# Rotation of the rotary vectors moved from TensorE to VectorE in blocks of 32 rows, and latent attention taken by pairs of heads

## The reference

```python
# differential attention, layer 1 of the first block: q and k have 8 heads x 2 maps x 64 values
q_l = apply_rope(rms_norm(q...), cos, sin); k_l = apply_rope(rms_norm(k...), cos, sin)
# latent attention (_mla), 8 heads, 16 meta tokens + 256 tokens = 272 positions
q = (_rmsnorm(q_lat, q_lat_w) @ w_uq).reshape(B, L, 8, 128 + 64)      # per head: 128 "nope", 64 rotary
kv = (_rmsnorm(kv_lat, kv_lat_w) @ w_ukv).reshape(B, L, 8, 128 + 128)
q_pe = _rope(_rmsnorm(q_pe, qpe_w), cos, sin)
k_pe = _rope(_rmsnorm(k_pe, kpe_w), cos, sin)                          # one rotary key for all heads
s = einsum(q_nope, k_nope) + einsum(q_pe, k_pe)
p = softmax(s * (128 + 64) ** -0.5); o = p @ v                         # then times silu(gate), out projection
# _rope / apply_rope on the halves x1, x2 (32 values each) of a 64-vector:
out = concatenate([x1 * cos - x2 * sin, x2 * cos + x1 * sin])
```

## Time and profile before

| | |
|---|---|
| median of 3 runs | 1290.42 us (1289.99 to 1291.06) |
| the profiled execution's own time | 1291.02 us |
| its span in the trace | 1289.3 us |
| mean granted TensorE clock | 0.984 of full speed |
| PE busy | 1225.1 us, 95% |
| DVE busy | 679.0 us, 53% |
| ACT busy | 549.8 us, 43% |

### The profile page before, as it was taken

One profiled execution on the slowest core, in us unless ns is written; L12 is line 12 of the kernel. 1 busy time (PEld: TensorE's weight loads), 2 busy tenths in 40 slices (PEclk: granted clock), 3 DMA queues, 4 the chain that ended last, 5 costly groups with the idle time before them and its releaser, 6 DMA issues.

```text
span 1289.3 us, 18951 instructions
## 1 busy us (share of the span) xinstructions
PE 1225.1 (95%) x7202; PEld 1002.7 (78%) x7202; DVE 679.0 (53%) x1141; ACT 549.8 (43%) x1026; POOL 87.2 (7%) x124
## 2 busy tenths in 40 slices
PE   7999999999999997999988899999899989999998
PEld 5765787787788885789946899999797675798467
DVE  3444477676433336555196754455664434355743
ACT  3234322222132224544366644444565554466742
POOL 0012011122000001000000200000100000020500
PEclk9999999999999998999989999999999999899899
DMA  9889265678422221323310465554353321363011
GB/s 326 307 309 325 87 196 184 198 263 277 155 98 98 92 87 50 98 77 121 99 34 1 131 196 191 174 184 152 123 179 100 96 89 45 75 201 142 33 43 56
DMA packets 121367, 183.40 MB, mean 142 GB/s; under 512 B 4305, under 2 KB 92672, under 8 KB 121296
## 3 DMA queue, kind: packets, MB, share of 16 engines
q1 hardware_dynamic: 113744, 154.64, 36.2%
q0 software_dynamic: 7552, 27.80, 6.8%
HBM read 181.37 MB, written 1.05 MB: 141 GB/s over the span
## 4 chain that ended last, share of the span: by engine, by line
PE 84%; DVE 7%; ACT 4%; issue 3%; POOL 1%; DMA 0%; DVEq 0%; SPq 0%; ACTq 0%; POOLq 0%
PE ps L440 20%; PE ps L442 20%; PE ps L441 20%; PE ps L751 2%; PE ps L791 2%; PE ps L752 2%; PE ps L753 2%; PE ps L920 2%; PE ps L933 2%; PE ps L1910 1%; PE ps L1954 1%; DVE wl L425 1%; PE ps L2242 1%; PE ps L2244 1%; PE ps L2243 1%
## 5 line engine op out<-in xcount | busy, mean ns | idle before, releaser
L425 DVE TENSOR_TENSOR wl<-raw,wh 128x1024 fp32r<-128x1024 f32 (+2 forms) x242 | 294.8, 1220 | 271.6 <-ACT wh L420 269.1
L440 PE MATMUL ps<-hh,wh 128*128 128x256 f32 (+3 forms) x1256 | 420.8, 335 | 17.1 <-DVE hl L570 11.4
L441 PE MATMUL ps<-hl,wh 128*128 128x256 f32 (+3 forms) x1256 | 412.1, 328 | 0.0
L442 PE MATMUL ps<-hh,wl 128*128 128x256 f32 (+3 forms) x1256 | 411.1, 327 | 0.0
L420 ACT ACTIVATE wh<-raw 128x1024 fp32r<-128x1024 f32 (+2 forms) x242 | 251.9, 1043 | 278.3 <-PE ps L442 256.5
L440 PEld LDWEIGHTS ps<-hh,wh 128*128 128x128 f32 (+1 forms) x1256 | 239.6, 191 | 57.3 <-issue 27.7
L442 PEld LDWEIGHTS ps<-hh,wl 128*128 128x128 f32 (+1 forms) x1256 | 239.7, 191 | 20.8
L441 PEld LDWEIGHTS ps<-hl,wh 128*128 128x128 f32 (+1 forms) x1256 | 238.9, 190 | 21.0 <-issue 0.2
L440 PE MATMUL ps<-ah,wh 128*128 128x256 f32 (+3 forms) x400 | 134.0, 335 | 5.5 <-DVE al L1751 3.0
L441 PE MATMUL ps<-al,wh 128*128 128x256 f32 (+3 forms) x400 | 131.9, 330 | 0.0
L442 PE MATMUL ps<-ah,wl 128*128 128x256 f32 (+3 forms) x400 | 131.7, 329 | 0.0
(11 more groups left out here) (209 smaller groups left out, 1474.8 us busy)
## 6 DMA issues: line engine op xcount, KB each, us to landing
raw<-in_ffn_w_in SPq DMA_DIRECT2D x44, 1024.0 KB, 5.1
raw<-in_ffn_w_out SPq DMA_DIRECT2D x22, 1024.0 KB, 4.9
raw<-in_w_in SPq DMA_DIRECT2D x22, 1024.0 KB, 5.4
big<-in_w_ada SPq DMA_DIRECT2D x16, 1024.0 KB, 9.7
big<-in_w_ada POOLq DMA_DIRECT2D x24, 512.0 KB, 4.4
ex<-in_w_ada POOLq DMA_DIRECT2D x24, 512.0 KB, 5.0
raw<-in_diff_w_in SPq DMA_DIRECT2D x12, 1024.0 KB, 5.1
raw<-in_w_out SPq DMA_DIRECT2D x8, 1024.0 KB, 4.9
```

Source lines behind the costliest of these rows:

```text
L425: nc.vector.tensor_tensor(split_half(wl, at), raw_half(at)[0], split_half(wh, at).bitcast(F32), ALU.subtract).then_inc(split, 1)
L440: nc.tensor.matmul(o, w_hi, m_hi, start=first, stop=False, **kw)
L441: nc.tensor.matmul(o, w_hi, m_lo, start=False, stop=False, **kw)
L442: return nc.tensor.matmul(o, w_lo, m_hi, start=False, stop=last, **kw)
```

## The change

It has two parts.

**Rotation.** The matmul with `rot` and its table go. The sine table gets its sign inside (`turn`). VectorE multiplies each block of 32 rows of the scaled vector by the sine rows and writes the product into the neighbouring block (0 to 1, 1 to 0, 2 to 3, 3 to 2), straight into the destination; then it multiplies by the cosine and adds. This holds for all units with rope.

**Pairs of heads.** The rotary parts of two heads become one unit of 128 features (heads 2f and 2f+1 on rows 0-63 and 64-127); the weights of a half are written in that order when they are rounded and split (`half_parts`, now two instructions for a half of `w_uq`). The rotary key is computed twice, on both row halves. `mla_pe`, `mla_act` and `mla_dve` replace the general attention code: 8 steps of two heads. Every step has four score products, a maximum over both, two exponentials, one scaling, four transposes and one transpose of 48 columns that holds the 16 meta columns of both heads (the odd head's keys stand meta first, 16 zero columns between); the value products of two heads follow each other with a third part of depth 48.

```diff
-    rot = np.zeros((P, P))
...
+    turn = np.where(np.arange(P) % 64 < 32, 1.0, -1.0)[:, None]
...
         def units_pe(pe, phase, h_base=None, before=0):
...
-                if 2 <= i and phase[i - 2].get("rope"):
...
-                    nc.tensor.matmul(ps[0:m, 5 + u["r"] % 2, 0:w], T["rot"][0:m, 0:m],
-                                     nrm[0:m, u["h"] % 2, 0:w], start=True, stop=True).then_inc(s_urot, 1)
...
         def units_dve(dve, link, mark, phase):
...
+                    for b in range(m // 32):
+                        to, at = slice(32 * b, 32 * b + 32), slice(32 * (b ^ 1), 32 * (b ^ 1) + 32)
+                        mark(nc.vector.tensor_tensor(turned[to], tile[at], T[sin][at, 0:w], ALU.mult))
                     link(nc.vector.tensor_tensor(t1[0:m, 0:w], tile, T[cos][0:m, 0:w], ALU.mult))
-                    dve.wait_ge(s_urot, u["r"] + 1)
-                    link(nc.vector.tensor_tensor(tile, ps[0:m, 5 + u["r"] % 2, 0:w], T[sin][0:m, 0:w],
-                                                 ALU.mult))
-                    nc.vector.tensor_tensor(u["dst"], t1[0:m, 0:w], tile, ALU.add).then_inc(s_urdy, 1)
+                    for r, n, place in places:
+                        ins = nc.vector.tensor_tensor(place, t1[r, n], turned[r, n], ALU.add)
+                    ins.then_inc(s_urdy, 1)
...
-        def query_units(h):
...
-            return [unit("head", q, 2, h % 2 * hd, P, L, 0, red="ones", dim=128, gain="qn", rope=None,
-                         out=[seg(qn[:, h, :], 0, L)], src=0),
-                    unit("head", q, 2, h % 2 * hd + P, MLA_ROPE, L, h % 2, red="ones", dim=64, gain="qpe",
-                         rope=("cos_m", "sin_m", L), out=[], dst=qp[0:MLA_ROPE, h, :], src=0)]
+        def query_units(f):
+            q = 2 * UQ_G[f // 2] + f % 2
+            return [unit("head", q, 2, j * MLA_NOPE, P, L, 0, red="ones", dim=128, gain="qn", rope=None,
+                         out=[seg(qn[:, 2 * f + j, :], 0, L)], src=0) for j in range(2)] + \
+                   [unit("head", q, 2, 2 * MLA_NOPE, P, L, 1, red="half", dim=64, gain="qpe",
+                         rope=("cos_m", "sin_m", L), out=[], dst=qp[:, f, :], src=0)]
...
-                a = query_units(4 * s) + query_units(4 * s + 1)
-                b = query_units(4 * s + 2) + query_units(4 * s + 3)
-                MLA_UNITS += a[:1] + [second] + a[1:3] + [third] + a[3:] + b[:3] + ahead + b[3:]
+                a, b = query_units(2 * s), query_units(2 * s + 1)
+                MLA_UNITS += a[:1] + [second] + a[1:2] + [third] + a[2:] + b[:2] + ahead + b[2:]
...
+        def mla_pe(pe, tail):
+            for i in range(MLA_STEPS + 4):
+                if i < MLA_STEPS:
+                    f, t = divmod(i, 2)
+                    q = slice(t * P, (t + 1) * P)
+                    if i >= 2:
+                        pe.wait_ge(s_ex, MLA_M0 + 2 * (i - 1))
+                    for c in range(2):
+                        nc.tensor.matmul(ps[:, (i % 2) * 2 + c, 0:L2], qn[:, 2 * f + c, q], kn[:, 2 * f + c, :],
+                                         start=True, stop=False)
+                    for c in range(2):
+                        r = slice(64 * c, 64 * c + 64)
+                        ins = nc.tensor.matmul(ps[:, (i % 2) * 2 + c, 0:L2], qp[r, f, q], kp[r, :],
+                                               start=False, stop=True)
+                    ins.then_inc(s_sc, 1)
...
+                if i % 2 == 0 and 0 <= (i - 4) // 2 < 4:
...
+                        for j in range(2):
+                            nc.tensor.matmul(o, mv[:, j, head], wT2[:, c, j, :],
+                                             start=(j == 0), stop=False)
+                        ins = nc.tensor.matmul(o, mv[0:32 + N_META, 2, head], wTm, start=False, stop=True)
...
+        def mla_dve(dve, link, mark):
+            for r in range(3):
+                link(nc.vector.memset(exm[:, r, L2:PAIR], 0.0))
```

More of the change, by code:

```diff
@@ L419, in round_half @@
             positive(act, used, q - SPLIT_SLOTS + 1)
-            nc.scalar.activation(split_half(wh, at), raw_half(at)[0], ACT.Copy).then_inc(rounded, 1)
+            for v, place in half_parts(at):
+                ins = nc.scalar.activation(place(wh), v, ACT.Copy)
+            ins.then_inc(rounded, 1)
         def split_low(dve, q, at):
             dve.wait_ge(rounded, q + 1)
-            nc.vector.tensor_tensor(split_half(wl, at), raw_half(at)[0], split_half(wh, at).bitcast(F32),
-                                    ALU.subtract).then_inc(split, 1)
+            for v, place in half_parts(at):
+                ins = nc.vector.tensor_tensor(place(wl), v, place(wh).bitcast(F32), ALU.subtract)
+            ins.then_inc(split, 1)
         def load_slab(sp, g, at, src, k, n):
@@ L635, in build @@
                                        dst=dv[:, t, s * 256:(s + 1) * 256]))
-        LAT_UNITS.append(unit("head", 2 * G["kpe"] + 1, KD, 0, MLA_ROPE, L2, 2, red="ones", dim=64,
-                              gain="kpe", rope=("cos_m", "sin_m", L2), out=[], dst=kp[0:MLA_ROPE, :]))
+        LAT_UNITS.append(unit("head", 2 * G["kpe"] + 1, KD, 0, P, L2, 2, red="half", dim=64,
+                              gain="kpe", rope=("cos_m", "sin_m", L2), out=[],
+                              dst=[(slice(0, 64), slice(0, L2), kp[0:64, :]),
+                                   (slice(64, P), slice(0, L), kp[64:P, N_META:L2]),
+                                   (slice(64, P), slice(L, L2), kp[64:P, 0:N_META])]))
         for m in range(2):
@@ L756, in unit_tile @@
                 m = slice(off, off + u["w"])
-                ins = product(o, tile_of(wh, at, 4, MLA_ROPE)[:, k % 4, :],
-                              tile_of(wl, at, 4, MLA_ROPE)[:, k % 4, :], mh[:, k, m], ml[:, k, m], first, last)
+                ins = product(o, tile_of(wh, at, 4, P)[:, k % 4, :], tile_of(wl, at, 4, P)[:, k % 4, :],
+                              mh[:, k, m], ml[:, k, m], first, last)
             else:
@@ L771, in units_pe @@
         def units_pe(pe, phase, h_base=None, before=0):
-            for i in range(len(phase) + 2):
+            for i in range(len(phase) + 1):
                 if i == 0 and h_base is not None:
@@ new lines, in mla_act @@
+        def mla_act(act):
+            for i in range(MLA_STEPS + 5):
+                if i < MLA_STEPS:
+                    act.wait_ge(s_mx, MLA_S0 + i + 1)
+                    if i >= 3:
+                        act.wait_ge(s_tr, MLA_S0 + i - 2)
+                    for c in range(2):
+                        nc.scalar.activation(exm[:, i % 3, c * PAIR:c * PAIR + L2], ps[:, (i % 2) * 2 + c, 0:L2],
+                                             ACT.Exp, bias=nm[:, i % 3, c:c + 1],
+                                             accum_out=sm[:, i % 3, c:c + 1]).then_inc(s_ex, 1)
+                if 2 <= i < MLA_STEPS + 2:
+                    j0 = i - 2
+                    f, t = divmod(j0, 2)
+                    act.wait_ge(s_tr, MLA_S0 + j0 + 1)
+                    if f >= 1:
+                        act.wait_ge(s_pv, MLA_H0 + f)
+                    nc.scalar.activation(wT2[:, :, :, t * P:(t + 1) * P],
+                                         ps[:, 4 + j0 % 2, :].rearrange("p (c j n) -> p c j n", c=2, j=2), ACT.Copy)
+                    nc.scalar.activation(wTm[:, t * P:(t + 1) * P], ps[0:32 + N_META, 7, 0:P],
+                                         ACT.Copy).then_inc(s_trc, 1)
+                if i % 2 == 0 and 0 <= (i - 6) // 2 < 4:
+                    o_round(act, A_MLA, (i - 6) // 2)
@@ L1553, in _ @@
             units_act(act, link, MLA_UNITS)
-            att_act(act, link, ATT["mla"])
+            mla_act(act)
             units_act(act, link, NA_GATE_UNITS)
@@ L1844, in _ @@
             dve.wait_ge(s_tab, 16)
-            units_dve(dve, link, DIFF_UNITS)
+            units_dve(dve, link, mark, DIFF_UNITS)
             att_dve(dve, link, mark, ATT["diff"])
```

150 lines of the change are left out of this document (107 added, 43 removed).

## The result

The changed kernel takes 1273.21 us (median of 4 runs, 1271.64 to 1273.77) where the kernel before takes 1290.29 beside it: a ratio of 0.9865, 95% interval 0.9852 to 0.9878, so 17.1 us faster. Forecast were 1270.5, with a range of 1265.5 to 1277.

A forecast was written before the change was run, and what follows sets the result against it. PE bounds the kernel (busy 95%, 84% of the chain), except where stages such as MLA_UNITS stall through DVE. Gains 1.8 + 0.4 + 7.9 + 7.1 + 2.8 = 20.0 from 1291.0 gave 1271.0, or 1270.5 against the median; range 1265.5 to 1277.

The forecast's parts named there:

- Part 1: DIFF_UNITS: 16 rotations leave PE (-6.9), but DVE becomes the bound in query units and PE waits 5.1; worth -1.8.
- the slack of 1.2: DIFF_UNITS query units: PE may run 1.2 to 1.6 ahead of the scaling before it waits; 1.2 was taken.
- Part 2: LAT_UNITS, the rotary key: one rotation leaves PE, -0.4; the added DVE work was costed at nothing.
- Part 3: MLA_UNITS: rotations and two rotary units leave PE, -3.5 a group, 1.6 of slow clock gone, 0.7 added; -7.9.
- the 1.6 for the clock: MLA_UNITS, second query group: half of 3.2 at half speed behind the second stall, counted as gone with its rotation.
- the rival of the moved stalls: MLA_UNITS gives 4 instead of 7 and one slow stretch returns behind another wait (1.6 to 2.8); 1276, chance 0.18.
- Part 4: Latent attention in steps of two heads, with row halves side by side and fewer waits: 44.3 against 51.4, -7.1.
- the waits at step 8 and at the end: Latent attention: third value product waits 1.4 for the copy; third gate unit behind the last values leaves 0.2.
- The clock behind the attention: After latent attention: the half-speed stretch of 5.6 behind the old wait goes with that wait, -2.8.
- overlap: Rotation products on DVE overlap at 0.34 each, so the DIFF_UNITS rotations give -4.8; 1267.5, chance 0.20.
- row halves that don't run side by side: Latent attention scores: each of 8 steps pays another 0.66 when a full product just wrote the bank; 1275.8, chance 0.12.
- the product across blocks: DIFF_UNITS query units: its price far above its columns makes the kernel slower, deciding near 0.97; 1304 at 1.2, chance 0.03.

The follow-up runs named there:

- the kernel with the queries on TensorE: Changed kernel, but the eight query units of DIFF_UNITS rotate on TensorE again, key units stay on VectorE: 1269.32 us, ratio 0.9831.
- the rotation alone: Kernel before, with rotation by VectorE on blocks of 32 rows everywhere and latent attention still head by head: 1295.31 us against 1291.23, ratio 1.003.
- the pairs alone: Changed kernel with every rotation on TensorE (DIFF_UNITS, rotary key, rotary units of MLA_UNITS): 1272.2 us, ratio 0.9852.
- The changed kernel's second trace: The changed kernel run once more, unedited, to stand beside two others on one chip: 1271.88 us, ratio 0.9842.
- the kernel with the gate unit ahead: Changed kernel with the third gate unit ahead of the last value products, as in the kernel before: 1278.03 us, ratio 0.9888.
- the four kinds of products: Changed kernel, DIFF_UNITS products varying by unit the block read or written, rotation left out: 1269.25 us in one run; only its rows count.
- the order of scores: Changed kernel with each head's row half right after its full-depth product, so the halves don't stand side by side: 1278.87 us, ratio 0.9898.

## Why the prediction was right, and where not

The time lies 2.7 above the forecast, near the upper end of the forecast's own range (1268 to 1273.5), and some of that is luck: part 1 missed by 3.4, parts 2 and 4 gave 1.8 more than forecast. What carries the forecast is the account of the pairs of heads, which the runs bear out.

**Part 1 (-1.8, measured +1.6) is the step that failed**, in the price and in the count. Products were 0.45 apart, not 0.42, and with them a unit took DVE 4.24, not 4.09. And I let only the last key unit count in the backlog, at the price of a query unit. Two of them fall under the shorter query units, at 4.63 each (two scalings; from one first scaling to the next in the kernel with the queries on TensorE) against 3.70 of PE. So DVE falls behind by 2 x 0.93 + 8 x 0.97 = 9.6, not 6.3. (The 6.3 was low by its own terms too: 0.82 a unit makes 6.6 over eight units and 7.4 over the nine that the text names.) Less the slack of 1.2 that I took, that is 8.4 of waiting. What the stage shows is 16 x 0.43 + 1.6 = 8.5. The key units gave what was forecast: sums 6.43 apart instead of 6.86, and the query sums were near 4.1 (4.24) without a gap on DVE. So the mechanism was seen and its size was not; had I counted all ten units, even at 0.42, part 1 would have come out at no gain. One reading of the four products was off without effect: the first of them changes only the block it reads, since it writes to block 0 as the scaling does.

**Part 2** (-0.4) gave 0.9. The mis-sized term is the price of the rotation. From the rotary key's sum to the first product with queries it is 38.23 before, 37.40 with the rotation alone, 37.74 with the pairs alone, and 37.31 with both. In the trace of before this rotation has 64 rows and takes 0.60 from its start to the next product (939.59 to 940.19), not the 0.43 of the earlier trace rows; so moving it gives 0.8 there, and with a key of 128 rows 0.4.

**Part 3** (-7.9) gave 7.3. The layout of the first group held: scaling of the rotary unit 13.6 behind the group's start where I had 14.2, the next group's first unit 19.4 where I had 19.7. The term that failed is the 1.6 for the clock. The second stall is shorter but not gone. The chain of the changed kernel:

```profile
1008.12 3.58 DVE wl L443 x3
1011.70 0.41 DVE nrm L870
```

and PE waits 0.96 for that scaling; behind it stands a slow stretch again:

```profile
1014.00:1016.00 2.00, 2.00 (x12) 2.00 (x11) 1.84 (x6) 0.00 (x0) 0.00 (x0) 0.50 0.67 230
```

That is the slow half of the rival of the moved stalls; its other half, 4 in place of 7, did not come. The changed kernel's second trace has the same wait (0.97) and no such stretch: the granted clock is 1.00 all through `MLA_UNITS`, which takes 83.0 instead of 84.5. Five other kernels with the same order of products and waits there took 82.9 to 83.0 as well, three 84.4 to 84.5. So the 1.6 is there in some traces and not in others, and what decides it stays open.

**Part 4** (-7.1) gave 8.4. A step's scores took 1.67 (1.7 forecast), the values of two heads 3.28 (3.36), the waits at step 8 and at the end 1.2 and 0.2 (1.4 and 0.2). The fifth transpose was mis-sized: the five take 0.60 (1069.42 to 1070.02 in the rows above), not 0.75, which makes 1.2 over eight steps.

**The clock behind the attention** (-2.8) gave 2.6, and the kernel with the gate unit ahead shows that wait and slow stretch belong together. Its size is not fixed: with the rotation alone the old wait is there (2.75), but the gate units behind it take 21.5, where they take 22.6 before and 19.95 without the wait.

Of the rivals, overlap fell with the four kinds of products, row halves that don't run side by side with the order of scores. None that would have made it slower had its price: the product across blocks costs 0.45, far from 0.97.

**Outside my sum** stand +2.0, -0.5 and -1.2, which make +0.3. The first is no work of the change (above). For the other two I find no cause but fewer microseconds at the lower clock: before, the three windows of 5 from 1190 to 1205 have 0.66, 0.50 and 0.82; in the changed kernel those from 1175 to 1190 have 0.69, 0.63 and 1.00. Why such a stretch is longer in one trace than in another stays open.

## What to carry to other kernels

Before work goes from the busiest engine to another, count the other engine's whole period per unit, in every unit whose work falls under the shorter ones, at the pitch that its instructions have there (0.45 here, not 0.34). Where that makes the other engine the slower one, move a part only: with the first six rotations moved and every second one of the last ten, both engines were level, and the stage was 4.3 shorter than with none moved and 5.8 shorter than with all. And a stage whose chain goes through waits gives back little of the work taken from the engine that waits: the rotations of `MLA_UNITS`, 0.43 or more each, gave 0.8 for four with the pairs, and next to nothing for eight without them.

## What the runs showed of the hardware

- On VectorE a change of the block of 32 rows, of the inputs or of the output, costs an instruction of 256 columns 0.11: 0.45 to the next one in place of 0.34.
- Products of two row halves of 64 take 0.66 together, and 0.65 each when a product of full depth stands between them, also where the bank was just written by a full product.
- PE's wait of 3.23 at the end of an attention is followed by a clock at the lower of its two levels for at least 4 of the next microseconds, with PE busy all the time; with a wait of 0.20 in its place the clock stays at 1.00.
- A wait of 0.96 or 0.97 at one and the same place in `MLA_UNITS` is followed by a stretch at the lower level in one trace of the changed kernel and by none in its second.
